# A hybrid decoder step on one core: TensorE's four head bodies become a loop of three and one copy

## The reference, cut to what matters

```python
def retention_chunkwise(q, k, v, s0):          # 4 heads, d=128, dv=256
    def step(s, qkv):
        qc, kc, vc = qkv
        inner = einsum('bihd,bjhd->bhij', qc, kc) * intra
        o = einsum('bhij,bjhe->bihe', inner, vc) + einsum('bihd,bhde->bihe', qc * q_decay, s)
        s = s * chunk_decay + einsum('bjhd,bjhe->bhde', kc * k_decay, vc)
        return s, o

def fox_sample(q, k, v, logf, k_past, v_past, logf_past):   # 8 samples, 4096 + 1 rows, 8 heads of 64
    c = cumsum(concatenate([logf_past, logf], 1), 1)
    s = concatenate([einsum('bqhd,bkhd->bhqk', q, k_past), einsum('bqhd,bkhd->bhqk', q, k)], -1) * scale
    p = softmax(s + c[:, p_len:] - c)
    return einsum('bhqk,bkhd->bqhd', p[..., :p_len], v_past) + einsum('bhqk,bkhd->bqhd', p[..., p_len:], v)

def reference(...):
    rq, rk, rv, rg, fq, fk, fv, lf, ga, gb = in_projection(xp, w_in, b_f, pos_p)
    ret_o, s_p = retention_chunkwise(rq, rk, rv, zeros)
    fox_o = fox_prompt(fq, fk, fv, lf)
    mix = merge_branches(ret_o, rg, fox_o, ga, gb, gn_w, gn_b, w_pa, w_pb, w_o)
    xp, c_p = post_norm_ffn(xp, mix, ...)       # LN, up / gate, causal convolution, gelu, down, LN
    # ... the same for the samples, with state_ret, state_conv and the paged cache
```

## Time and profile before

| | us |
|---|---|
| median of 3 runs | 2202.43 |
| lowest, highest | 2200.81, 2207.22 |
| the profiled execution, its own time | 2207.22 |
| its span (first to last instruction) | 2205.6 |
| `retain` heads 1 to 4, from the profile | 184.4, 180.3, 181.5, 126.5 |

### The profile page before, as it was taken

One profiled execution on the slowest core, in us unless ns is written; L12 is line 12 of the kernel. 1 busy time (PEld: TensorE's weight loads), 2 busy tenths in 40 slices (PEclk: granted clock), 3 DMA queues, 4 the chain that ended last, 5 costly groups with the idle time before them and its releaser, 6 DMA issues.

```text
span 2205.6 us, 39738 instructions
## 1 busy us (share of the span) xinstructions
PE 2007.4 (91%) x14335; PEld 1870.7 (85%) x14335; DVE 1160.8 (53%) x1771; ACT 645.5 (29%) x1175; POOL 239.6 (11%) x269
## 2 busy tenths in 40 slices
PE   7998998688998999899879899799999999999996
PEld 6887887677886888787769799599999999999995
DVE  4644546855865875786432765833322333233356
ACT  4444443123222223312320100534411332023333
POOL 1000000110020020011000010400000000000034
PEclk9999999899998999899979999799999999999998
DMA  4111113685886688598552321011111111111143
GB/s 134 50 39 40 39 39 118 201 311 174 271 304 223 228 300 275 174 315 293 182 173 72 129 72 35 19 48 48 45 51 39 48 48 42 54 48 38 52 131 133
DMA packets 135014, 277.59 MB, mean 126 GB/s; under 512 B 19105, under 2 KB 38686, under 8 KB 134870
## 3 DMA queue, kind: packets, MB, share of 16 engines
q1 hardware_dynamic: 96914, 168.84, 22.5%
q0 software_dynamic: 25184, 89.75, 13.8%
q10 hardware_dynamic: 12800, 17.40, 2.2%
HBM read 247.77 MB, written 28.25 MB: 125 GB/s over the span
## 4 chain that ended last, share of the span: by engine, by line
PE 42%; DVE 5%; DMA 2%; issue 1%; ACT 1%; DVEq 0%; POOL 0%; SPq 0%; ACTq 0%; POOLq 0%
PE bank L121 39%; PE bank L1584 2%; DMA w_raw<-in_w_down_dram 1%; DVE x_lo L1798 1%; DMA gated_raw<-gated_t_scratch 1%; DVE chunk_tmp L1727 0%; DVE w_lo L104 0%; DVE chunk_tmp L1729 0%; DVE z L1795 0%; DVE y L1844 0%; DVE merged_hi L1731 0%; PE banks L1542 0%; DVE moving_lo L1733 0%; DVE ln_stats L1853 0%; DMA z<-fox_t_scratch 0%
## 5 line engine op out<-in xcount | busy, mean ns | idle before, releaser
L121 PE MATMUL bank<-x_hi,w_hi 128*128 128x344 f32 (+1 forms) x1944 | 639.9, 329 | 50.3 <-DVE x_lo L1798 15.0
L121 PE MATMUL bank<-x_lo,w_hi 128*128 128x344 f32 (+1 forms) x1944 | 629.6, 324 | 0.0
L121 PE MATMUL bank<-x_hi,w_lo 128*128 128x344 f32 (+1 forms) x1944 | 629.4, 324 | 0.0
L121 PEld LDWEIGHTS bank<-x_hi,w_hi 128*128 128x128 f32 (+1 forms) x1944 | 370.5, 191 | 68.8 <-issue 57.0
L121 PEld LDWEIGHTS bank<-x_lo,w_hi 128*128 128x128 f32 (+1 forms) x1944 | 370.8, 191 | 1.6
L121 PEld LDWEIGHTS bank<-x_hi,w_lo 128*128 128x128 f32 (+1 forms) x1944 | 370.5, 191 | 1.7
L97 ACT ACTIVATE w_hi<-w_raw 128x1024 fp32r<-128x1024 f32 (+3 forms) x161 | 163.0, 1013 | 573.3 <-PE bank L121 368.4
L121 PE MATMUL bank<-moving_hi,w_hi 128*128 128x344 f32 x744 | 229.5, 330 | 25.9 <-DVE moving_lo L1709 14.2
L104 DVE TENSOR_TENSOR w_lo<-w_raw,w_hi 128x1024 fp32r<-128x1024 f32 (+3 forms) x161 | 192.7, 1197 | 103.8 <-ACT w_hi L97 90.5
L121 PE MATMUL bank<-moving_lo,w_hi 128*128 128x344 f32 x744 | 239.3, 322 | 0.0
L121 PE MATMUL bank<-moving_hi,w_lo 128*128 128x344 f32 x648 | 209.7, 324 | 0.0
(11 more groups left out here) (263 smaller groups left out, 2761.8 us busy)
## 6 DMA issues: line engine op xcount, KB each, us to landing
cache_keys<-in_cache_k_dram SPq DMA_DIRECT2D x256, 256.0 KB, 4.8
cache_vals<-in_cache_v_dram SPq DMA_DIRECT2D x256, 256.0 KB, 5.2
w_raw<-in_w_in_dram POOLq DMA_DIRECT2D x52, 512.0 KB, 5.9
w_raw<-in_w_down_dram POOLq DMA_DIRECT2D x32, 448.0 KB, 4.5
w_raw<-in_w_up_dram POOLq DMA_DIRECT2D x22, 512.0 KB, 4.5
w_raw<-in_w_gate_dram POOLq DMA_DIRECT2D x22, 512.0 KB
gate<-gate_t_scratch SPq DMA_DIRECT2D x16, 516.0 KB, 3.5
gate_t_scratch<-rot_cos ACTq DMA_DIRECT2D x24, 172.0 KB, 4.0
```

The lines of the kernel that those rows point to most:

```text
L121: mm = pe.matmul(g.bank[n][0:m, 0:TC], w[slot][:, k, 0:m], x[:, k, chunk(n)], start=(k == 0 and i == 0), stop=(k == kt - 1 and i == 2))
```

## The change

PE runs its heads through the helper that the other engines use. The loop's three laps take `h` from a register; the fourth head is a copy with constants, as before.

```diff
@@ -1048,8 +1048,7 @@
                         product(g, pe, job(h * NJ + J0, 1, NJ + 3), g.xh, g.xl, after=ending)
                     pe.wait_ge(rn_out, (h + 1) * 2 * NB)
-                for h in range(RH):
-                    body(h, h == RH - 1)
+                heads(pe, body)
```

## The result

| | us |
|---|---|
| before, median of 8 runs | 2204.14 (2197.07 to 2209.68) |
| after, median of 8 runs | 2214.64 (2212.49 to 2226.46) |
| ratio, with its 95% interval | 1.0055 (1.0037 to 1.0074) |

The change makes the kernel slower, by 0.55% or 12.1 us (8.2 to 16.3) of 2204; the two medians of the table differ by 10.5. Another 22 runs of the changed kernel are on record, from 2207.10 to 2224.26 us, and they give the same ratio. The prediction had said 2204.4, and no change as the likeliest: its whole range, 2199 to 2216, holds the measured time, but the forecast's own, 2200 to 2209, does not. The rival that it called "the cover does not hold" had said 2214.8.

The account below looks back on a forecast made before the run. The prediction took TensorE (PE) to bound the kernel, busy for 2007.4 of 2205.6 us. Seams 0 plus register operations 2.0 took the median from 2202.4 to 2204.4; the range was 2199 to 2216, the forecast's own 2200 to 2209.

Parts of the forecast that it names:

- the cover does not hold: Rival: late PE delays DVE's split_lo, keys, SP and all landings at the bursts at 645 and 661; 12.4 us, 2214.8, chance 0.22.
- The jump: PE's taken branch at two seams of retain's heads: 6.0 us, of which 2.6 is queued work, leaving a 3.5 us hole.
- The clock: Behind each hole PE's clock falls to its lower level: 1.7 us added per seam, up to 3.3.
- PE late by 5.2 into each head: Hole plus clock fall delay PE at the start of heads 2 and 3, by 5.2 us each; bounds 1.4 and 6.8.
- What it meets: Early in heads 2 and 3, waits for cached values (6.1 and 5.4 us) take in PE's lateness; both seams cost 0.
- the cover: PE's waits for cached values in a head's first 50 us, taken to absorb 5.2 us; without them both seams cost 10.4.
- What a late PE holds up: In PE's next head, ACT's copies, ACT's split_hi and DVE's split_lo come later by as much; DVE's keys stand behind.
- Register operations: 50 register rows a lap on PE over three laps, partly hidden: 2.0 us, bounds 0 and 6.8.
- Removed, and the exit: PE executes as many instructions as before; the branch passed after the third lap takes 0.08 us, within the queue's cover.
- The jump is cheap: Rival: prefetch or placement spares the fetch at PE's seams, no hole at 617, only register operations stay; 2204.4, chance 0.10.
- placement: Rival: PE's code behind the loop gets other addresses and a loop of finish misses every lap; 10 us, 2214, chance 0.05.
- The clock gains: Rival: shorter waits spare clock falls, both seams give back 1.7 and register operations are hidden; -3.4, 2199.0, chance 0.08.

Follow-up runs that it names:

- The half dose: 14 overwritten matmuls added on PE ahead of heads 2 and 3 of the kernel before, which has no loop there: 1.0029, 2208.35 us.
- five kernels: PE's heads written out with h in a register (1.0025), and four hinted loops of heads (1.0007, 1.0006, 0.9987, 0.9996), each against the kernel before.
- the run made for it alone: Kernel before with PE's heads still written out, but h a register in the first three, so register operations without a branch: 1.0025, 2208.1 us.
- the hinted kernels: Prefetch hint on PE's heads loop: changed kernel 1.0007, with DVE's hint too 0.9987; two-lap loop with heads 3 and 4 written out 1.0006.

## Why the prediction was wrong, step by step

*The jump* (6.0 us forecast, hole 3.5): 6.74 and 6.30, holes 4.26 and 3.82. Right, a little low. DVE's row of the same seam was the better bound than `fox`'s.

*The clock* (1.7, up to 3.3): PE went from 4.5 us late at the end of the first hole to 7.0 ten microseconds on, so 2.5 for the clock; at the second from 4.1 to 5.6, so 1.5. Right.

*PE late by 5.2 into each head* (1.4 to 6.8): 7.0 and 5.6. Low, and the first just outside the bounds.

*What it meets: "The values' landings do not move, because SP's pace is its own."* This is the step that failed: the cover, costed at 0 for both seams where the two heads together measured some 12 us. The burst of loads that began at 645.75 began at 655.16, 7.0 us later counted from the seam. I had read SP's waits (0.7 us, all for DVE) as slack, but a wait of 0.7 says that DVE was already the later of the two, and a stretch of 630 to 672 left out the wait of 4.2 us at the seam. DVE had little room as well: it reached `split_lo` at 633.71, 1.4 us behind `split_hi`'s end at 632.35. So the room was 1.4, not the pause of 6.

*What a late PE holds up.* I named the right chain (ACT's copies, `split_hi`, `split_lo`, DVE's keys behind) and then let it go with "DVE too waits for DMA in this stretch". That wait was for keys which SP loads when DVE frees a slot. In a ring whose slots are freed by the two engines that wait, a wait for DMA is cover only until the late loads arrive. The half dose shows it (6.4 for 4.4). So do the heads behind a jump: the waits took in 3.4 us in the first 53 us, and 2.4 of them came back later.

*Register operations* (2.0, 0 to 6.8): 0 to 2 by the mean of five kernels; the run made for it alone says 5.5 (1.5 to 9.5).

*Removed, and the exit:* nothing. The passed branch took 0.08 us.

*The rivals.* "The cover does not hold" had place (the burst at 645), price (12.4) and link right: 12.1 measured. That the price is so near is partly luck: PE was 12.6 us late over both seams and not 10.4, the waits took in a little, and the register operations cost less than 2.0. "The jump is cheap" and "placement" fall by the traces and by the hinted kernels. "The clock gains" falls: the longest wait for values in head 2 grew from 2.31 to 3.75 us. The forecast and this rival differed in one question, whether the waited-for loads hang on the engine that waits, and the profile of before pointed to the answer: SP's only waits there were for DVE, 4.9 us from 616 to 672.

## What to carry to other kernels

Before a wait for a DMA is counted as cover for a delay, follow the ring round: who issues the load, what frees its slot, and what stands ahead of that on the freeing engine. If the delayed engine is in that chain with less room than the delay, what the wait takes in comes back at a later one. The long loop body on TensorE cost a stop at each taken branch, with all that follows about 6 us here and 12 in all; a prefetch hint at its top costs 0.03 us and removed it.

## What was not expected of the hardware

- The same kind of jump had different prices: 3.4 to 4.5 us in the attention stage, 6.0 to 7.5 in `retain`, over all kernels without a hint. The DMA share around the two differs (0.17 from 195 to 215 us against 0.96 in the earlier trace rows); whether that is why was not tried.
- DVE's stop at the seam was not dearer when PE stood still at the same time: 5.3 us at both seams after, 5.98 before. DVE's own branch row (line 777) is 0.08 us at most; its stop shows only as idle time behind it, where PE's lies within the branch's row.
- The hint on DVE took away 6 us of standing at each seam and gave nothing (0.9999).
